# Differential attention on one core: groups of two heads become units of one head, interleaved at a distance of one unit

## The reference, cut to what matters

```python
def diff_attend(q, k, v, lam):
    s = jnp.einsum('bqhcd,bkhcd->bhcqk', q, k).astype(jnp.float32) * (q.shape[-1] ** -0.5)
    p = jax.nn.softmax(s, axis=-1)
    w = p[:, :, 0] - lam * p[:, :, 1]
    return jnp.einsum('bhqk,bkhe->bqhe', w.astype(v.dtype), v)
...
    ox = (rmsnorm(ox, subln_g) * (1.0 - lam_init)).reshape(B, L, D_MODEL) @ w_out
```

## Time and profile before

| | us |
|---|---|
| median of three runs | 1975.62 (1974.87 to 1977.59) |
| the profiled execution | 1977.56, its span 1975.8 |
| PE busy in it | 1820.3 (92%) |
| DVE, ACT busy | 475.0, 386.9 |
| mean granted TensorE clock | 0.952 |
| last product before the second attention to first product of the output projection | 803.8 to 909.5 |

### The profile page before, as it was taken

One profiled execution on the slowest core, in us unless ns is written; L12 is line 12 of the kernel. 1 busy time (PEld: TensorE's weight loads), 2 busy tenths in 40 slices (PEclk: granted clock), 3 DMA queues, 4 the chain that ended last, 5 costly groups with the idle time before them and its releaser, 6 DMA issues. The chain is left out here.

```text
span 1975.8 us, 35831 instructions
## 1 busy us (share of the span) xinstructions
PE 1820.3 (92%) x16214; PEld 1069.0 (54%) x16214; DVE 475.0 (24%) x762; ACT 386.9 (20%) x662; POOL 34.8 (2%) x71
## 2 busy tenths in 40 slices
PE   5999789999999889865799999999999999999995
PEld 2743478888888768544535345353443534435342
DVE  3313445222233663454310100101001010010103
ACT  3223433222232432342100000100001000010001
POOL 1000100000000000000000000000000000000000
PEclk8998899999999999987699999999999999999997
DMA  9255462332324232347599999999999999999970
GB/s 372 96 171 171 144 187 72 99 100 93 107 86 138 69 109 84 129 150 271 228 339 367 369 363 375 327 364 373 368 361 335 364 371 361 368 334 365 369 294 24
DMA packets 141160, 477.43 MB, mean 242 GB/s; under 512 B 11168, under 2 KB 35096, under 8 KB 122576
## 3 DMA queue, kind: packets, MB, share of 16 engines
q1 hardware_dynamic: 137344, 467.64, 64.5%
q0 software_dynamic: 3664, 7.48, 1.2%
HBM read 473.96 MB, written 1.13 MB: 240 GB/s over the span
## 5 line engine op out<-in xcount | busy, mean ns | idle before, releaser
L950 PE MATMUL ps<-w_hi,h_t 128*128 128x512 f32 (+1 forms) x960 | 298.2, 391 | 18.9 <-DVE h_t L1532 7.2
L950 PE MATMUL ps<-w_moe,h_te 128*32 128x256 f32 (+1 forms) x3520 | 296.6, 493 | 16.4 <-DVE residual L1876 16.4
L950 PE MATMUL ps<-h_t,w_hi 128*128 128x512 f32 (+1 forms) x768 | 222.5, 374 | 5.0 <-DVE h_t L1532 5.0
L950 PEld LDWEIGHTS ps<-w_moe,h_te 128*32 128x32 f32 x3520 | 113.2, 111 | 193.3 <-issue 138.9
L950 PE MATMUL ps<-w_raw,h_te 128*32 128x256 f32 (+2 forms) x3648 | 216.8, 396 | 0.0
L1479 DVE TENSOR_TENSOR w_lo<-w_raw,w_hi 128x2048 fp32r<-128x2048 f32 x58 | 132.9, 2292 | 349.0 <-ACT w_hi L619 348.5
L950 PEld LDWEIGHTS ps<-w_hi,h_t 128*128 128x128 f32 x960 | 182.6, 193 | 59.7 <-issue 8.3
L950 PE MATMUL ps<-w_lo,h_t 128*128 128x512 f32 (+1 forms) x480 | 186.9, 389 | 0.0
L1875 DVE TENSOR_TENSOR residual<-silu_g,ps 128x512 f32<-128x512 f32 (+1 forms) x32 | 19.8, 618 | 650.7 <-ACT silu_g L894 650.7
L619 ACT ACTIVATE w_hi<-w_raw 128x2048 fp32r<-128x2048 f32 x58 | 110.8, 1914 | 327.9 <-PE ps L950 319.4
L950 PEld LDWEIGHTS ps<-w_raw,h_te 128*32 128x32 f32 x3648 | 112.2, 110 | 100.9 <-issue 61.5
(11 more groups left out here) (233 smaller groups left out, 1213.6 us busy)
## 6 DMA issues: line engine op xcount, KB each, us to landing
w_moe<-in_expert_in_w_dram SPq DMA_DIRECT2D x110, 1024.0 KB, 6.2
w_raw<-in_expert_out_w_dram SPq DMA_DIRECT2D x62, 1024.0 KB, 7.1
w_raw<-in_expert_in_w_dram SPq DMA_DIRECT2D x50, 1024.0 KB, 7.7
w_raw<-in_ada_w_dram SPq DMA_DIRECT2D x48, 1024.0 KB, 5.0
w_moe<-in_expert_out_w_dram SPq DMA_DIRECT2D x34, 1024.0 KB, 7.0
work<-in_expert_in_w_dram SPq DMA_DIRECT2D x32, 1024.0 KB, 7.2
w_raw<-in_expert_in_w_dram SPq DMA_DIRECT2D x64, 512.0 KB, 4.8
w_raw<-in_ffn_in_w_dram SPq DMA_DIRECT2D x44, 512.0 KB, 4.9
```

The lines of the kernel that those rows point to most:

```text
L950: return pe.matmul(out_, l, r, start=first, stop=last, skip_group_check=True)
```

## The change

The attention is cut into sixteen **units** u of one head and one query tile. A unit has two maps. It uses banks 0 and 1 or 2 and 3 for its scores, bank 4 or 5 for its transposes and one half of the old `PT1`, by the parity of u; bank 6 holds one output. Scores run two units ahead (`scores1(u+2)` waits for the exponentials of u), the values of u-1 come behind the transposes of u, and each turn has one `ada` block at its end instead of two at its start.

The combination leaves the maps unnormalised: with sums s1 and s2, it makes e1 - (lambda s1 / s2) e2 in one `scalar_tensor_tensor` per head, and the factor 1/s1 is applied by ACT as the `scale` of the output's copy and square. The two normalising multiplications of a group are gone.

The side work keeps its kind but moves: `ada_rows(4)` stands in DVE's turn 8, `sqrt(0, 8)` behind the exponentials of unit 12 on ACT, `sub_norm(0)` in DVE's turn 11, `ada_rows(5)` behind all units; and three blocks of the projection's weights are split inside the loop, behind turns 13, 14 and 15, where it was two.

```diff
-        def exps1(g):
-            act.wait_ge(negmax, 8 + g + 1)
-            if g:
-                act.wait_ge(p_tr, 24 + 2 * g)
-            for j in range(4):
+        def exps1(u):
+            p = 2 * (u % 2)
+            act.wait_ge(negmax, U0 + u + 1)
+            if u >= 2:
+                act.wait_ge(p_tr, T0 + u - 1)
+            for j in range(p, p + 2):
...
+        def output1(u):
+            t, h, r = u // 8, u % 8, 2 * (u % 4)
+            act.wait_ge(pv_done, U0 + u + 1)
+            act.activation(OA[:, t, P * h:P * h + P], ps[:, 6, 0:P], ACT.Copy, scale=RL[:, r:r + 1])
+            if u:
+                act.wait_ge(o_raw, u)
+            act.activation(T2[:, 0:P], ps[:, 6, 0:P], ACT.Square, scale=RL[:, r:r + 1],
+                           accum_out=SS[:, u:u + 1]).then_inc(o_raw, 1)
...
+        exps1(1)
+        for u in range(U1):
+            p = u % 2
+            act.wait_ge(p_tr, T0 + u + 1)
+            if u >= 2:
+                act.wait_ge(pv_done, U0 + u - 1)
+            act.activation(PT2[:, p, :, :], ps[:, 4 + p, :].rearrange("p (c q) -> p c q", c=4),
+                           ACT.Copy).then_inc(pt_even if p == 0 else pt_odd, 1)
+            if u:
+                output1(u - 1)
+            if u < U1 - 2:
+                exps1(u + 2)
+            if u == 10:
                 sqrt(0, 8)
-            if g >= 6:
-                hi_upto(B_DOUT + g - 5)
+            if u >= 13:
+                hi_upto(B_DOUT + u - 12)
+        output1(U1 - 1)
...
+        for u in range(U1):
+            p = u % 2
+            if u < U1 - 2:
+                pe.wait_ge(exps, U0 + u + 1)
+                scores1(u + 2)
+            pe.wait_ge(prob_scaled, U0 + u + 1)
+            if u >= 2:
+                pe.wait_ge(pt_even if p == 0 else pt_odd, C0 + u // 2)
+            for c_ in range(4):
+                ins = pe.transpose(ps[:, 4 + p, c_ * P:(c_ + 1) * P], P1[:, 2 * p, c_ * P:(c_ + 1) * P], ID[:])
+            ins.then_inc(p_tr, 1)
+            if u:
+                values1(u - 1)
+            ada(4 * DK + u)
+        values1(U1 - 1)
...
-            link(dve.reciprocal(RL[:], SUMS[:]))
-            link(dve.tensor_scalar(NRL[:], RL[:], LAM[:, 0:1], None, ALU.mult))
-            for hh in range(2):
-                ins = dve.tensor_scalar(P1[:, 2 * hh, :], P1[:, 2 * hh, :], RL[:, 2 * hh:2 * hh + 1], None, ALU.mult)
...
+        def combine1(u):
+            p, r = 2 * (u % 2), 2 * (u % 4)
+            dve.wait_ge(exps, U0 + u + 1)
+            link(dve.reciprocal(RL[:, r:r + 2], SUMS[:, p:p + 2]))
+            link(dve.tensor_scalar(NRL[:, p:p + 1], RL[:, r + 1:r + 2], LAM[:, 0:1], SUMS[:, p:p + 1],
+                                   ALU.mult, ALU.mult))
+            dve.scalar_tensor_tensor(out=P1[:, p, :], in0=P1[:, p + 1, :], scalar=NRL[:, p:p + 1], in1=P1[:, p, :],
+                                     op0=ALU.mult, op1=ALU.add).then_inc(prob_scaled, 1)
...
+        for u in range(U1):
+            if u < U1 - 2:
+                maxima1(u + 2)
+            if u < U1 - 1:
+                combine1(u + 1)
+            if u == 8:
+                ada_rows(4)
+            if u >= 13:
+                lo_upto(B_DOUT + u - 12)
+            if u == 11:
+                dve.wait_ge(o_raw, 8)
                 sub_norm(0)
-        dve.wait_ge(o_raw, 8)
+        ada_rows(5)
+        dve.wait_ge(o_raw, U1)
         sub_norm(1)
```

More of the change, by code:

```diff
@@ L76 @@
 SPLIT_AHEAD = 2
+U0 = 8
+T0 = 24
+C0 = 12
+U1 = 16
 ADA_ATT0 = [3, 3, 2, 2, 2, 2, 2, 0]
@@ L496, in experts @@
             if rnd == 0:
-                sp.wait_ge(scores, 16)
+                sp.wait_ge(scores, U0 + U1)
                 for n in range(RING):
@@ L582, in _ @@
         mod_rows(2)
[L583 removed]
+        pool.wait_ge(pv_done, U0)
         gate_rows(0)
@@ L1223, in _, with scores1 @@
                 nat_transposes(0)
-        def scores1(g):
-            t, hp = g // 4, g % 4
-            if g:
-                pe.wait_ge(exps, 8 + g)
-            else:
-                pe.wait_ge(nat_evac, 4)
-            for j in range(4):
-                h, p0 = 2 * hp + j // 2, HD * (j % 2)
-                ins = mm(ps[:, j, :], QT1[p0:p0 + HD, h, t * P:(t + 1) * P], KT1[p0:p0 + HD, h, :], True, True)
+        def scores1(u):
+            t, h, p = u // 8, u % 8, 2 * (u % 2)
+            if u >= 2:
+                pe.wait_ge(exps, U0 + u - 1)
+            for j in range(2):
+                ins = mm(ps[:, p + j, :], QT1[HD * j:HD * j + HD, h, t * P:(t + 1) * P],
+                         KT1[HD * j:HD * j + HD, h, :], True, True)
             ins.then_inc(scores, 1)
+        pe.wait_ge(nat_evac, 4)
         pe.wait_ge(v_even, 1)
@@ L1663, in _ @@
             dve.wait_ge(exps, g + 1)
-            link(dve.tensor_tensor(RL[:], SUMS[:], ES[:], ALU.add))
-            link(dve.reciprocal(RL[:], RL[:]))
+            link(dve.tensor_tensor(RL[:, 0:4], SUMS[:], ES[:], ALU.add))
+            link(dve.reciprocal(RL[:, 0:4], RL[:, 0:4]))
             for j in range(4):
@@ L1731, in _, with maxima1 @@
         dve.sem_inc(lam_dve, 1)
[L1732 to L1735 removed]
+        def maxima1(u):
+            p = 2 * (u % 2)
+            dve.wait_ge(scores, U0 + u + 1)
+            link(dve.tensor_reduce(MX[:, p:p + 2], ps[:, p:p + 2, :], AX_X, ALU.max))
+            dve.tensor_scalar(NEGM[:, p:p + 2], MX[:, p:p + 2], -SCALE, None, ALU.mult).then_inc(negmax, 1)
         def sub_norm(t):
```

81 lines of the change are left out of this document (14 added, 67 removed).

## The result

| | before | after |
|---|---|---|
| median of the runs, us | 1975.24 (1972.54 to 1977.59, 4 runs) | 1953.8 (1950.3 to 1956.94, 4 runs) |
| ratio, 95% interval | | 0.9891 (0.987 to 0.9913) |
| span of the profiled run, us | 1975.8 | 1952.0 |

The change takes 1.1% off, 21.4 us between the medians; 18.7 were forecast. To compare traces I use a length that does not depend on where the stage begins: **the stage**, from the first scores product of the second attention to the first product of the output projection. (The 803.8 in the table ahead is that first scores product, not the product before it.) It was 105.73 us before (803.76 to 909.49) and is 84.23 after (801.64 to 885.87): 21.5 less, which is the difference of the medians. Of the remaining 2.3 us between the two profiled runs 2.1 lie in front of the stage, where the programs do the same work, and 0.2 behind it.

A forecast was written before the change was run, and what follows sets the result against it. DVE and ACT wait for each other, PE for both; the change makes PE the bound. Ten 3.8 us units with start, clock and rows reach 851.85, plus 38.95 puts the projection at 890.8, 18.7 earlier: 1957 us, range 1949 to 1969.

The forecast's parts named there:

- rival C: Behind the attention: the gain is lost because the experts' DMA stream does not start earlier; 1975 us, chance 0.05.
- PE's unit: Attention loop: PE takes 3.8 us per unit, against 8.07/2 = 4.03 before; lower bound 3.5, uncertainty 3.5 to 4.1.
- start, first waiting scores behind the first scores: Start of second attention: the chain shrinks from four maps to two, first waiting scores at 810.05 against 812.48.
- lower clock at the start: First turns: PE, idle nearly 5 us before, runs at its lower level; 3.1 us charged, uncertainty -3 to +1.
- `ada_rows(4)` before block 40: Turn 8: PE's block 40 waits for DVE's adaptive rows, +1.8 us; before the change they cost nothing.
- block three's load landed: Tail: the third weight block's load takes 5.1 us, landing 25.95 us after turn 10; up to 9 if others queue.
- cheaper start of the projection: Projection's own start at the lower clock level could shorten, as PE idles less before it; 0 to -2 us.
- The hole around the root: Sign in the loop: ACT and DVE show a hole around the first tile's square root.
- ACT waiting 5 us for block three's load: Sign in the tail: ACT waits about 5 us for the load of the third weight block.
- A: Loop: one unit's chain sets the pace, as if distance were one; 4.75 us per unit, +15, 1972 us, chance 0.10.
- B: Loop: PE at the lower clock, 7.5 us per unit instead of 3.8; 2016 us if all sixteen, chance 0.04.
- D: Loop and start: PE's unit at 3.5 and full clock at the start, -5 - 3; 1949 us, chance 0.11.

The follow-up runs named there:

- e3: Kernel after with maps normalised as before, one more DVE multiplication per unit and no scale on ACT's output; 1956.72 us, stage 85.52.
- e7: Kernel after with adaptive rows first in turn 8, weight blocks split in turns 9, 11 and 14, root and norm in turn 14; 1948.85 us, stage 82.82.
- e8: e7 with two adaptive blocks moved ahead of turn 0 and `ada_rows(4)` moved to turn 6; 1951.34 us, stage 82.69.
- e1: Kernel after with the third weight block split behind the `z_t` copies again, as before the change; 1956.59 us, ratio to before 0.9912, stage 89.52.
- e2: Kernel before the change, with only the splits of the second and third weight block moved ahead of the last output; 1964.42 us, ratio 0.9953, stage 96.39.
- e4: Kernel after with scores, maxima and exponentials one unit ahead instead of two; 1977.36 us, ratio to before 1.0021, stage 105.92.
- e6: Kernel after with the first tile's root and norm moved behind the last exponentials; 1952.02 us (1 run), stage 85.08.
- e9: Kernel after with half the products of adaptive blocks 1 to 14 left out, output not the reference's; 1952.64 us (1 run), stage 84.37.
- e12: Kernel after run again unchanged, as partner of two other runs on the same chip; 1952.45 us, stage 84.40.

## Why the prediction was right

**The mechanism** held in its parts, and the end followed the stage (21.5 and 21.4 us), so rival C, the gain lost behind, is refuted. Over all kernels with more than one timed execution the difference to before in the time was within 3.4 us of that in the stage.

**The mis-sized term is PE's unit**: 3.8 forecast, 3.53 measured. The working set 3.5 as the lower bound, from half of PE's rows of a group, and added 0.07 to each of the four kinds for a fixed head and tail, 0.28 in all. Both were too high. A row's length contains the end of its last product, but the next kind starts under it; what counts is the distance of starts. By starts a group without its two pauses is 8.07 - 0.35 - 0.83 = 6.89 us, not 7.02, and its half 3.45. The rows of a unit start 1.06, 0.50, 0.98 and 1.00 apart, 3.54 in all, 0.09 more than that half: values halve exactly (1.96 to 0.98), while a block takes 1.00 where two took 1.85. Over the ten turns to turn 10 this is 2.7 us, nearly the whole of 21.5 - 18.7.

**The other terms**, measured from the same points:

| term | forecast | measured |
|---|---|---|
| start, first waiting scores behind the first scores | 6.3 (810.05 - 803.76) | 6.52 |
| lower clock at the start | 3.1 | 2.95 (turns 0 and 1 take 9.03, at 3.53 each and without values in turn 0 they would take 6.08) |
| `ada_rows(4)` before block 40 | 1.8 | 1.81 |
| last exponentials end, behind turn 10 (847.36) | 16.65 | 16.53 |
| block one's low part ends | 20.8 | 20.65 |
| block three's load landed | 25.95 | 25.7 |
| its low part ends | 30.2 | 29.9 |
| output transposes | 33.7 | 33.27 |
| projection | 38.95 | 38.51 |

Turn 10's scores came at 847.36; corrected for a stage that starts 2.12 earlier, the forecast was 849.73. The 2.4 us there and 0.4 behind make the 2.8 us.

Two agreements owe something to luck. The lower clock at the start cost 2.95 us in this trace for 3.1 forecast, but in e3, e7 and e8 only 1.5 to 1.6 (turns 0 and 1 in 7.58 to 7.69 us). And the chance for a cheaper start of the projection, 0 to 2 us, came to 0.5: from the projection's first product to the router's transposes are 34.29 us, for 34.83 before.

**The split of the gain** was 7.8 in the loop and 10.9 behind; it was 10.4 and 11.1. e1 gives the third block's place 5.3 of the latter by its trace and some 4.3 without the clock's share, with the 11.2 and 5.25 us from transposes to projection that were forecast (11.21 and 5.24 measured); e2 gives the second and third block's place 8.6 in the old loop, so the parts don't simply add up.

**Points of the list.** The hole around the root is there: `std` at 854.83 and the table load at 856.15, turn 12 takes 4.75. ACT waiting 5 us for block three's load is not: it waits 0.25 for the load itself, because the copy of unit 15 and the output of unit 14, with ACT's waits of 1.81 and 1.11 for PE, fill the time, and DVE waits 3.63 for the high part. The load's 5.04 us (868.03 to 873.07) are a link of the path all the same: low part of block one, load, high part, low part, norm. The list called the forecast wrong if a load sets the last 20 us, while its own sum had the load as such a link. e1 says how much hangs on it: with the block out of that path the transposes came only 0.7 us earlier, 2.1 with the clock's 1.4 set aside, as the last values and the root come not much sooner. GpSimd's rows cost nothing that a trace shows: issued at 885.39, they are first used at 897.48, without a wait for the load.

**Rivals.** A, the distance of one: e4 shows what it would have been, 4.99 us a turn for 4.75, with the waits of 1.39 and 2.39. B, the lower clock: 1.00 from 820 to 863 us. The Trainium skill, page "TensorE: Matmul & The Clock Gate", section "A second HAM failure mode: psum-queue depth-cycling", tells of a kernel in which cycling through PSUM banks gave PE short pauses so often that its clock swung between the two levels. This trace does not agree: the banks are cycled twice as often and the clock stays at 1.00. But an ordinary turn has no pause of PE either, so the run does not test what many short pauses would do; where the clock fell inside the loop, a single pause stood before it (2.27 us in e3, 3.18 in e7, 4.04 in e4). D, PE's unit at 3.5, was right in that term and wrong in the other: the lower clock at the start stayed.

## What to carry to other kernels

Where an in-order loop over several engines has each of them waiting in turn, put one piece of distance between producer and consumer on every engine; smaller pieces alone make it worse (4.99 us against half of 8.07). Cost the new bound by the distance between starts, with the surcharge that rows show and no more (0.09 us a unit here, where 0.28 was put in), and then look for the one-off jobs on the other engines: such a loop has only their small waits in reserve (0.94 us here), and a job of 2 us in the wrong place of an engine's queue stops it (1.8 us for the rows, 3.2 for a weight block). A job that stands behind the last step of its own chain, like the split of the third block, is worth about its whole length (some 4.3 us in e1, for a high and a low part of 4.2 together), whatever the loop does.

## What the hardware showed that I had not expected

- A short pause can be enough for the lower level. In e3 PE waited 2.27 us and then ran two kinds of work at half speed; in the kernel after it waited 1.81 at the same place and did not, nor in e1, e6, e9 and e12, which had that wait too. In e7 the level fell after a wait of 3.18, in e8 after one of 2.58 at the start. In these windows of e3 (stretch, length, busy PE, clock, DMA share, GB/s) the granted clock falls and returns within 4 us:
```profile
840.00:844.00 4.00, 2.14 (x16) 1.00 0.92 292
844.00:846.00 2.00, 1.59 (x8) 0.59 0.13 46
846.00:848.00 2.00, 2.00 (x8) 0.55 0.39 64
848.00:850.00 2.00, 2.00 (x19) 1.00 0.89 344
```
- How long it lasts is not fixed by the program. After the same pause at the stage's start the lower level held until 814.3 in the kernel after, 12.6 us after the first scores, and in e7 until 814.9, 9.5 after them; turn 0 took 4.54 and 3.10 us. The same holds at the stage's end (e1). Two stages that differ by 1 to 2 us are therefore to be compared turn by turn, with the granted clock beside each.
- Products on separate groups of 32 columns cost nothing beside each other: two of four left out, the block still took 1.05 us (e9).
